# Sample queries spread per head inside the query product of a decoder trunk

## The chip, the cores and the metric

The kernel runs on one core of a Trainium2 chip. The core has five engines that run their own instruction lists and meet only at semaphores: PE (matrix products into PSUM banks), DVE and ACT (elementwise work), POOL and SP (here they mostly issue transfers). The metric is the device time of one launch in microseconds. Of the kernel before there are three runs: 1816.34, 1818.75 and 1823.96 us, median 1818.75 us.

## The reference, cut to what matters

Two token groups pass the same two layers: 256 prompt tokens and 8 sample tokens (one each of 8 sequences). Each layer has a token mixer, a cross attention over 256 memory tokens with 4 heads of 256 columns, and a channel mixer (dense, then eight experts). The prompt attends to keys computed in the kernel; each sample token attends to a cache of its own, read from memory:

```python
def cross_attention(h, k, v, w_q, w_o):
    b, s, _ = h.shape
    q = (h @ w_q).reshape(b, s, XATTN_HEADS, XATTN_HEAD_DIM)
    scores = jnp.einsum('bshd,bmhd->bhsm', q, k) * (XATTN_HEAD_DIM ** -0.5)
    p = jax.nn.softmax(scores, axis=-1).astype(v.dtype)
    o = jnp.einsum('bhsm,bmhd->bshd', p, v).reshape(b, s, D_MODEL)
    return o @ w_o

y_prompt = trunk(x_prompt, mem_k_prompt, mem_v_prompt, ...)   # 256 tokens, one memory
y_sample = trunk(x_sample, cache_mem_k, cache_mem_v, ...)     # 8 tokens, caches (2, 8, 256, 4, 256)
```

A layer's sample caches are 8 MB of keys and 8 MB of values. All data is fp32.

## The kernel before, in words

All 264 tokens (`T` = `TP` + `TS` = 256 + 8) are held transposed, features on the 128 partitions. Weights come in pieces of 1 MB through a ring of six slots (`raw`); ACT rounds a piece to fp32r (`whi`), DVE takes the remainder (`wlo`, in `split`), and PE multiplies hi by hi, hi by lo and lo by hi (`product`). `split(n + SPLIT)` for a piece three ahead stands in ACT's and DVE's lists behind the work on piece n. The order of each engine is the order of the code.

A layer's attention begins with the query product: four pieces, one head each (`q0` or `q1`, in `normed_product`). After the first piece stands a channel sum for the RMS norm (`channel_sum`, line 684). DVE scales each piece into `qT` (`q_out`, line 1657). Small results go through PSUM banks 4 to 7 in turn, by a running job number (`AUX`, `aux`, `job_out`): a job waits until the job four before it has been read.

Then, before the change, in this order:
- PE turns the sample queries into rows (`q_tok`), ACT copies them to `qs`; PE makes the prompt scores (`scores`, line 805), DVE takes their maxima (lines 1667, 1670), ACT the exponentials into `pr` (line 1223) and later the scaled `pr` (line 1231).
- For each sample s and each half of the columns PE spreads a query row over all partitions (`q_bc`, line 813: a column of the identity, held over 128 columns, times `qs`, 8 rows deep), and DVE multiplies it with the keys and sums (line 1685, four instructions a job, one for each head and half of the memory). There are 16 such jobs and 64 such instructions in a layer.
- PE turns the sample scores (`s_t`) and the prompt's probabilities (`p_t`), forms the prompt's output (`o_t`, line 838), and, with the values scaled by ACT (line 1248) and summed by DVE (line 1710), the samples' output (`s_o`, line 846). The product `o0` or `o1` follows.

POOL issues the cache loads (`load_caches`, line 505), 1 MB each, one sample's keys or values, in runs of 4 KB. Keys go through a ring of three slots (`kv`); values through it as well and through `va` (over `qT`) and `vb` (over `kT`), each of these two used twice in a layer.

Of the kernel before, what the change touches and what calls it, by code (L numbers as in the profile page):

```python
# [12 lines left out]
P = 128  # L13
# [3 lines left out]
TS = 8  # L17
# [106 lines left out]
for _c in range(CH):  # L124
    EP += [("g", _c, 0), ("g", _c, 1), ("u", _c, 0), ("u", _c, 1)]
    if _c:
# [16 lines left out]
_ATT = [("rms_xatt", 1), ("q_tok", 2), ("scores", 4), ("q_bc", 16), ("s_t", 1), ("p_t", 4), ("ps_t", 1), ("o_t", 4),  # L143
        ("s_o", 2), ("os_t", 1)]
for _name, _count in (
    [("vec", 1), ("mem_t", 4), ("x_t", 8), ("ws_t", 2), ("ws_0", 1), ("rms_mix0", 1), ("k_tok0", 4), ("ln_a0", 1), ("ln_b0", 1),
     ("v_smp", 2), ("v_tok", 4), ("mixed", 4)] + [(n + "0", c) for n, c in _ATT]
    + [("rms_ffn0", 1), ("rms_mix1", 1), ("state_t", 4), ("pconv", len(PE_CONV)), ("k_tok1", 4), ("ln_a1", 1), ("ln_b1", 1), ("c_tok", 4)]
    + [(n + "1", c) for n, c in _ATT] + [("ya", 3), ("route", 1), ("yb", 3), ("pos", 2)]
):  # L150
    AUX[_name] = _n
    _n += _count

# [31 lines left out]
def build_step(nc, ctx, a, out):  # L185
# [12 lines left out]
    def sem(name):  # L198
        return ctx.enter_context(nc.semaphore(name))
# [50 lines left out]
    vb = at("vb", [P, 2, D], F32, c_off + 8192)  # L250
    sc = at("sc", [P, 2, TS * HEADS], F32, e_off + 45312)
# [81 lines left out]
    v_scaled, v_summed, va_in, vb_in = sem("v_scaled"), sem("v_summed"), sem("va_in"), sem("vb_in")  # L333
# [57 lines left out]
    def key_slot(i, s):  # L391
        return ring_slot(12 * i + s)

    def value_slot(i, s):
        if s in (0, 5):
            return va[:, :, :], (va_in, 16 * (2 * i + s // 5 + 1))
        if s in (1, 6):
            return vb[:, :, :], (vb_in, 16 * (2 * i + s // 6 + 1))
        return ring_slot(12 * i + 8 + (2, 3, 4, 7).index(s))
# [5 lines left out]
    def job_out(name, j=0):  # L405

        n = AUX[name] + j
        return aux_free[n % 4], n // 4 + 1

    def job_bank(name, j=0):  # L410
        return bank[4 + (AUX[name] + j) % 4]
# [65 lines left out]
    def _(pool):  # L477
# [23 lines left out]
        def load_caches(i):  # L501

            def load(cache, s, place):
                dst, (loaded, _) = place
                pool.dma_start(dst, a[cache][i, s].rearrange("(m p) h d -> p m (h d)", p=P)).then_inc(loaded, 16)

            for s in range(TS):
                if s == 3:
                    pool.wait_ge(aux_ready, AUX[f"scores{i}"] + 4)
                    load("cache_mem_v", 0, value_slot(i, 0))  # L510
                    load("cache_mem_v", 1, value_slot(i, 1))
                if s >= 3:
                    pool.wait_ge(*job_out(f"q_bc{i}", 2 * (s - 3) + 1))
                elif i == 1 and s < 2:
                    pool.wait_ge(vused, s + 4)
                elif i == 1:
                    pool.wait_ge(aux_ready, AUX["s_o0"] + 2)
                load("cache_mem_k", s, key_slot(i, s))
            for s in range(2, TS):
                if s < 5:  # L520
                    pool.wait_ge(*job_out(f"q_bc{i}", 2 * (s + 3) + 1))
                else:
                    pool.wait_ge(vused, (TS - 1) * i + s - 4)
                load("cache_mem_v", s, value_slot(i, s))
# [109 lines left out]
    def _(pe):  # L634
        def aux(name, j=0):

            n = AUX[name] + j
            if n >= 4:
                pe.wait_ge(aux_free[n % 4], n // 4)
            return bank[4 + n % 4]  # L640
# [150 lines left out]
        def attention(i):  # L791
            normed_product(f"q{i}", 4, f"xatt{i}")
            pe.wait_ge(*stage_out(f"q{i}", 4))
            for j in range(2):
                y = aux(f"q_tok{i}", j)
                for kk in range(4):
                    mm = turn(y[0:TS, kk * P:(kk + 1) * P], qT[:, 4 * j + kk, TP:T], P)
                mm.then_inc(aux_ready, 1)
            for j in range(4):
                y = aux(f"scores{i}", j)  # L800
                tt, hh = j // 2, j % 2
# [6 lines left out]
            pe.wait_ge(*job_out(f"q_tok{i}", 0))  # L808
            pe.wait_ge(*job_out(f"q_tok{i}", 1))
            for s in range(TS):  # L810
                for c in range(2):
                    y = aux(f"q_bc{i}", 2 * s + c)
                    pe.matmul(y[:, :], ident[0:TS, s:s + 1].to_broadcast([TS, P]), qs[:, c * 512:(c + 1) * 512],  # L813
                              start=True, stop=True).then_inc(aux_ready, 1)
# [5 lines left out]
            for j in range(4):  # L820
                tt, mt = j // 2, j % 2
                y = aux(f"p_t{i}", j)
                pe.wait_ge(p_done, 4 * i + 2 * tt + 2)
# [259 lines left out]
    def _(act):  # L1083
# [24 lines left out]
        def job_copy(name, j, dst, rows_=P, cols=512):  # L1108
            act.wait_ge(aux_ready, AUX[name] + j + 1)
# [102 lines left out]
        def attention(i):  # L1212
            normed_pieces(f"q{i}", 4, f"xatt{i}")
            if i == 1:
                act.wait_ge(stored, 16 * 4)
            for j in range(2):
                job_copy(f"q_tok{i}", j, qs[:, j * 512:(j + 1) * 512], TS)
            for j in range(4):
                tt, hh = j // 2, j % 2
# [7 lines left out]
            for j in range(4):  # L1227
                act.wait_ge(rsum_done, 4 * i + j + 1)
                for h2 in range(2):
                    tt, h = j // 2, 2 * (j % 2) + h2  # L1230
# [224 lines left out]
    def _(dve):  # L1455
# [22 lines left out]
        def job_copy(name, j, dst, rows_=P, cols=512):  # L1478
            dve.wait_ge(aux_ready, AUX[name] + j + 1)
# [173 lines left out]
        def attention(i):  # L1653
# [6 lines left out]
            normed_pieces(f"q{i}", 4, f"xatt{i}", q_out)  # L1660
            if i == 1:
                dve.wait_ge(stored, 16 * 4)
            for j in range(4):
                tt, hh = j // 2, j % 2
                c = 4 * tt + 2 * hh
                dve.wait_ge(aux_ready, AUX[f"scores{i}"] + j + 1)
# [3 lines left out]
                dve.tensor_scalar(att[:, 8 + c:10 + c], att[:, c:c + 2], -SCALE, None, ALU.mult).then_inc(nmax_done, 1)  # L1670
            for j in range(4):
                tt, hh = j // 2, j % 2
# [3 lines left out]
            for s in range(TS):  # L1676
                keys, loaded = key_slot(i, s)
                dve.wait_ge(*loaded)
                for c in range(2):
                    j = 2 * s + c  # L1680
                    dve.wait_ge(aux_ready, AUX[f"q_bc{i}"] + j + 1)
                    for h in (2 * c, 2 * c + 1):
                        for mt in range(2):
                            k = keys[:, mt, h * HD:(h + 1) * HD]
                            ins = dve.tensor_tensor_reduce(k, k, job_bank(f"q_bc{i}", j)[:, (h % 2) * HD:(h % 2 + 1) * HD],
                                                           1.0, 0.0, ALU.mult, ALU.add,
                                                           sc[:, mt, s * HEADS + h:s * HEADS + h + 1])
                    ins.then_inc(job_out(f"q_bc{i}", j)[0], 1)
# [425 lines left out]
```

## Time and profile before

| | |
|---|---|
| median of three runs | 1818.75 us (1816.34 to 1823.96) |
| profiled execution | 1817.56 us, its span 1815.8 us |
| mean granted TensorE clock | 0.967 of full |
| busy share of the span | PE 95%, DVE 77%, ACT 59%, POOL 4% |
| chain that ended last | PE 90%, DVE 5%, ACT 2%, DMA 2% |
| attention of layer 0, from the channel sum's end to the first matmul of `o0` | 177.46 to 263.48 us |
| attention of layer 1, the same | 692.60 to 779.34 us |

The share of busy time counts PE as busy while a matmul waits in its pipeline, and the two attentions make up under a tenth of the span. So the stretches that the change touches are read by themselves: the chain of waits says in order of time which engine's work ended last, the timeline gives the length of single instructions and the distance between their starts, and the windows give the granted clock of a stretch.

### The profile page before, as it was taken

The page shows a single profiled execution, that of the slowest core. Times are in us where ns is not written, and L with a number is a line of the kernel's source. Part 1 is how long each engine was busy: PE and PEld are TensorE (multiplying, and loading weights), DVE is VectorE, ACT ScalarE, POOL GpSimd, SP SyncE. Part 2 cuts the span into 40 slices and gives each one's busy share as a digit, 9 for nine tenths or more (in the row PEclk, how much of TensorE's full clock was granted, in tenths as well). Part 3 has the DMA queues.
Part 4 walks back from the last instruction along what each step waited for, and adds up shares of the span by engine and source line. Part 5 has one row for each costly group of instructions (what it writes and reads, how often), then busy time and mean ns, then how long its engine had stood idle before and what let it go on. Part 6 is the DMA issues. An engine that isn't in the chain of part 4 may idle for free.

```text
span 1815.8 us, 23483 instructions
## 1 busy us (share of the span) xinstructions
PE 1733.5 (95%) x9598; PEld 1476.6 (81%) x9598; DVE 1400.5 (77%) x1635; ACT 1079.6 (59%) x1051; POOL 76.9 (4%) x86
## 2 busy tenths in 40 slices
PE   7998989999999989998999999999999999999996
PEld 6988659999999878486888888888888888888875
DVE  6566756665588966646888988988889889888896
ACT  4543344443454445335777777777777777777764
POOL 0000110000000000110000000000000000000000
PEclk9999789999999989688999999999999999999998
DMA  9644744555752345635999999999999999999993
GB/s 327 212 162 165 274 167 149 179 178 172 222 186 73 116 165 189 252 117 201 371 380 378 380 369 380 374 374 383 370 376 380 367 385 371 377 381 371 378 384 110
DMA packets 286375, 505.91 MB, mean 279 GB/s; under 512 B 8295, under 2 KB 100807, under 8 KB 285717
## 3 DMA queue, kind: packets, MB, share of 16 engines
q1 hardware_dynamic: 271904, 449.41, 70.1%
q0 software_dynamic: 13856, 54.75, 8.1%
q8 instruction: 78, 1.28, 0.3%
q14 instruction: 37, 0.30, 0.0%
q10 hardware_dynamic: 500, 0.18, 0.0%
HBM read 491.93 MB, written 13.33 MB: 278 GB/s over the span
## 4 chain that ended last, share of the span: by engine, by line
PE 90%; DVE 5%; ACT 2%; DMA 2%; issue 1%; ACTq 0%; DVEq 0%; POOLq 0%
PE bank L1028 17%; PE bank L1030 17%; PE bank L1029 16%; PE bank L668 9%; PE bank L669 9%; PE bank L670 9%; PE bank L692 3%; PE bank L735 2%; PE bank L684 2%; PE bank L813 1%; PE bank L838 1%; PE bank L661 1%; PE bank L663 1%; PE bank L662 1%; PE bank L805 1%
## 5 line engine op out<-in xcount | busy, mean ns | idle before, releaser
L1907 DVE TENSOR_TENSOR wlo<-raw,whi 128x2048 fp32r<-128x2048 f32 x333 | 761.9, 2289 | 110.1 <-ACT whi L1364 109.2
L1364 ACT ACTIVATE whi<-raw 128x2048 fp32r<-128x2048 f32 x333 | 638.6, 1918 | 211.0 <-PE bank L1030 211.0
L1028 PE MATMUL bank<-whi,xeh 128*128 128x512 f32 x896 | 360.9, 403 | 1.8 <-DVE wlo L1907 1.2
L1030 PE MATMUL bank<-whi,xel 128*128 128x512 f32 x896 | 352.5, 393 | 0.0
L1029 PE MATMUL bank<-wlo,xeh 128*128 128x512 f32 x896 | 349.0, 390 | 0.0
L668 PE MATMUL bank<-xh,whi 128*128 128x264 f32 (+1 forms) x1056 | 306.3, 290 | 19.0 <-DVE xl L1537 8.0
L1466 DVE TENSOR_TENSOR wlo<-raw,whi 128x2048 fp32r<-128x2048 f32 (+1 forms) x93 | 211.7, 2276 | 141.7 <-ACT whi L1096 141.3
L669 PE MATMUL bank<-xl,whi 128*128 128x264 f32 (+1 forms) x1056 | 302.4, 286 | 0.0
L670 PE MATMUL bank<-xh,wlo 128*128 128x264 f32 (+1 forms) x1056 | 302.1, 286 | 0.0
L1096 ACT ACTIVATE whi<-raw 128x2048 fp32r<-128x2048 f32 (+1 forms) x93 | 175.8, 1891 | 163.2 <-PE bank L670 161.7
L668 PEld LDWEIGHTS bank<-xh,whi 128*128 128x128 f32 x1056 | 202.2, 191 | 20.8 <-issue 16.3
L669 PEld LDWEIGHTS bank<-xl,whi 128*128 128x128 f32 x1056 | 202.4, 192 | 0.3
L670 PEld LDWEIGHTS bank<-xh,wlo 128*128 128x128 f32 x1056 | 201.5, 191 | 0.0
L1030 PEld LDWEIGHTS bank<-whi,xel 128*128 128x128 f32 x896 | 168.8, 188 | 39.2
L1028 PEld LDWEIGHTS bank<-whi,xeh 128*128 128x128 f32 x896 | 169.2, 189 | 34.8 <-DVE wlo L1907 2.5
L1029 PEld LDWEIGHTS bank<-wlo,xeh 128*128 128x128 f32 x896 | 169.2, 189 | 34.4
L1028 PE MATMUL bank<-whi,hTh 128*128 128x512 f32 x448 | 176.8, 395 | 1.9 <-DVE hTl L1949 1.9
L1030 PE MATMUL bank<-whi,hTl 128*128 128x512 f32 x448 | 175.6, 392 | 0.0
L1029 PE MATMUL bank<-wlo,hTh 128*128 128x512 f32 x448 | 174.0, 388 | 0.0
L1028 PEld LDWEIGHTS bank<-whi,hTh 128*128 128x128 f32 x448 | 84.2, 188 | 19.9 <-DVE wlo L1907 2.3
L1030 PEld LDWEIGHTS bank<-whi,hTl 128*128 128x128 f32 x448 | 84.1, 188 | 19.6
L1029 PEld LDWEIGHTS bank<-wlo,hTh 128*128 128x128 f32 x448 | 84.1, 188 | 18.6
(314 smaller groups left out, 1870.2 us busy)
## 6 DMA issues: line engine op xcount, KB each, us to landing
raw<-in_moe_w_gate SPq DMA_DIRECT2D x112, 1024.0 KB, 6.3
raw<-in_moe_w_up SPq DMA_DIRECT2D x112, 1024.0 KB, 6.9
raw<-in_moe_w_down SPq DMA_DIRECT2D x112, 1024.0 KB, 6.8
kv<-in_cache_mem_k POOLq DMA_DIRECT2D x16, 1024.0 KB, 5.5
raw<-in_b_w_pw SPq DMA_DIRECT2D x12, 1024.0 KB, 5.2
raw<-in_ffn_w_gate SPq DMA_DIRECT2D x11, 1024.0 KB, 5.3
raw<-in_ffn_w_up SPq DMA_DIRECT2D x11, 1024.0 KB, 5.3
raw<-in_w_xk SPq DMA_DIRECT2D x8, 1024.0 KB, 9.0
```

The source lines that it names most:

```text
L668: pe.matmul(y, w_hi[:, cols], x_hi, start=first, stop=False)
L669: pe.matmul(y, w_hi[:, cols], x_lo, start=False, stop=False)
L670: mm = pe.matmul(y, w_lo[:, cols], x_hi, start=False, stop=last)
L684: mm = pe.matmul(y[:, 0:T], ones[:, :], src[:, k, :], start=(k == order[0]), stop=(k == order[-1]))
L692: return pe.transpose(dst, src, ident[0:rows_, 0:rows_])
L1028: pe.matmul(y[:, :], x_hi, w_hi, start=starts, stop=False)
L1029: pe.matmul(y[:, :], x_hi, w_lo, start=False, stop=False)
L1030: mm = pe.matmul(y[:, :], x_lo, w_hi, start=False, stop=stops)
L1096: act.activation(whi[:, n % SPLIT, 0:w], raw[:, n % RAW, 0:w], ACT.Copy).then_inc(hi_done, 1)
L1364: act.activation(whi[:, n % SPLIT, :], raw[:, n % RAW, :], ACT.Copy).then_inc(hi_done, 1)
L1466: dve.tensor_tensor(wlo[:, n % SPLIT, 0:w], raw[:, n % RAW, 0:w], whi[:, n % SPLIT, 0:w].bitcast(F32), ALU.subtract).then_inc(lo_done, 1)
L1907: dve.tensor_tensor(wlo[:, n % SPLIT, :], raw[:, n % RAW, :], whi[:, n % SPLIT, :].bitcast(F32), ALU.subtract).then_inc(lo_done, 1)
```

## The change

The 16 spreading jobs are no longer one for each sample and half, but four for each head, two samples each, and they stand inside the query product: after pieces 1, 2 and 3 of it PE spreads the head of the piece before, and the last head between the two pairs of prompt scores. A job is now a 128x128 matrix of ones times four 128x128 diagonals (`dq`), which ACT writes from `qT` (64 instructions in a layer; the identity scaled by a column). `q_tok` and its copies to `qs` fall away. DVE's 64 score instructions are the same in number and size, and follow their head's spreading. The prompt scores go by pairs of heads, in order (head pair, token tile). Keys are loaded per head and four samples (1 MB, now in runs of 1 KB); values of samples 3 to 6 have the homes `va`, `vb`, `vc` (over `pr`) and `vm` to themselves, and 0, 1, 2 and 7 go through the ring.

```diff
-_ATT = [("rms_xatt", 1), ("q_tok", 2), ("scores", 4), ("q_bc", 16), ("s_t", 1), ("p_t", 4), ("ps_t", 1), ("o_t", 4),
-        ("s_o", 2), ("os_t", 1)]
+_ATT = [("rms_xatt", 1), ("q_bc", 12), ("scores_l", 2), ("q_bd", 4), ("scores_r", 2), ("s_t", 1), ("p_t", 4), ("ps_t", 1),
+        ("o_t", 4), ("s_o", 2), ("os_t", 1)]
...
+    vc = at("vc", [P, 2, D], F32, sq_off)
+    dq = at("dq", [P, 4, 4, P], F32, e_off + 8448)
...
+    def keys_free(i, r):
+        return job_out(f"q_bc{i}", 4 * (r // 2) + 2 * (r % 2) + 1)
...
     def value_slot(i, s):
...
+        if 3 <= s <= 6:
+            place, loaded = ((va, va_in), (vb, vb_in), (vc, vc_in), (vm, vd_in))[s - 3]
+            return place[:, :, :], (loaded, 16 * (i + 1))
+        return ring_slot(12 * i + 8 + (0, 1, 2, 7).index(s))
...
# POOL, load_caches
+            for r in range(8):
+                h, half = r // 2, r % 2
+                if r >= 3:
+                    pool.wait_ge(*keys_free(i, r - 3))
...
+            for s in range(TS):
+                if s < 3:
+                    pool.wait_ge(*keys_free(i, s + 5))
+                elif s < 5:
+                    pool.wait_ge(aux_ready, job_no(f"scores{i}", 3) + 1)
+                elif s == 5:
+                    pool.wait_ge(aux_ready, job_no(f"p_t{i}", 3) + 1)
+                elif s == 6:
+                    pool.wait_ge(vm_out, 16 * (i + 1))
+                    pool.wait_ge(aux_ready, job_no(f"o_t{i}", 3) + 1)
+                else:
+                    pool.wait_ge(vused, (TS - 1) * i + 1)
...
# PE, attention
+            def spread(h):
+                for jj in range(4):
+                    j = 4 * h + jj
+                    y = aux(f"q_bc{i}", j)
+                    pe.wait_ge(dq_done, 16 * i + j + 1)
+                    pe.matmul(y[:, :], ones[:, :], dq[:, jj, :, :].rearrange("p b n -> p (b n)"),
+                              start=True, stop=True).then_inc(aux_ready, 1)
...
+            for h in range(HEADS - 1):
+                product(f"q{i}", 1, x_hi, x_lo, start=h + 1)
+                spread(h)
...
+            scores(0)
+            scores(1)
+            spread(HEADS - 1)
+            pe.wait_ge(*stage_out(f"q{i}", 4))
+            scores(2)
+            scores(3)
...
# ACT, attention
+            def spread_rows(n):
+                h = n - FIRST[f"q{i}"]
+                act.wait_ge(*tile_out(n, 1))
+                for jj in range(4):
+                    j = 4 * h + jj
+                    if h > 0:
+                        act.wait_ge(aux_ready, job_no(f"q_bc{i}", j - 4) + 1)
+                    for b in range(4):
+                        s = 2 * jj + b // 2
+                        ins = act.activation(dq[:, jj, b, :], ident[:, :], ACT.Copy,
+                                             scale=qT[:, 2 * h + b % 2, TP + s:TP + s + 1])
+                    ins.then_inc(dq_done, 1)
...
+            for h in range(1, HEADS):
+                pieces(f"q{i}", 1, start=h)
+                spread_rows(FIRST[f"q{i}"] + h)
...
# DVE, attention
+            for h in range(HEADS):
+                n = FIRST[f"q{i}"] + h
+                q_out(n)
+                if h > 0:
+                    sample_scores(h - 1)
+                split(n + SPLIT)
+            largest(0)
+            largest(1)
+            sample_scores(HEADS - 1)
+            largest(2)
+            largest(3)
```

PE's list in layer 0, from the last prompt scores (`kT,qT`) on, before: the spreading jobs (`qs,ident`) stand one behind the other after all four scores.

```order
L805 MATMUL bank<-kT,qT 128x256 [waits aux2_free]
L805 MATMUL bank<-kT,qT 128x256 x3
L805 MATMUL bank<-kT,qT 128x256 [waits aux3_free]
L805 MATMUL bank<-kT,qT 128x256 x3
L813 MATMUL bank<-qs,ident 128x512 [waits aux0_free,aux3_free,aux2_free]
L813 MATMUL bank<-qs,ident 128x512 [waits aux1_free]
```

The same place after the change, from the third head's last two spreading jobs (`dq,ones`) on:

```order
L815 MATMUL bank<-dq,ones 128x512 [waits dq_done,aux0_free]
L815 MATMUL bank<-dq,ones 128x512 [waits dq_done,aux1_free]
L825 MATMUL bank<-kT,qT 128x256 [waits aux2_free,bank3_evac]
L825 MATMUL bank<-kT,qT 128x256 x3
L825 MATMUL bank<-kT,qT 128x256 [waits aux3_free]
L825 MATMUL bank<-kT,qT 128x256 x3
L815 MATMUL bank<-dq,ones 128x512 [waits dq_done,aux0_free]
L815 MATMUL bank<-dq,ones 128x512 [waits dq_done,aux1_free]
L815 MATMUL bank<-dq,ones 128x512 [waits dq_done,aux2_free]
L815 MATMUL bank<-dq,ones 128x512 [waits dq_done,aux3_free]
L825 MATMUL bank<-kT,qT 128x256 [waits aux0_free,bank3_evac]
```

The first three heads' jobs have moved ahead of the scores, and the last head's third and fourth job now wait for the banks (`aux2`, `aux3`) that hold the first two scores.

POOL's list in layer 0 from the fourth key load on, before (`kv`, `va`, `vb` are the places; `aux` banks come free when DVE has used a spread query, `vused` rises when PE has used a sample's values):

```order
L505 DMA kv<-in_cache_mem_k 128x2x1024 [waits aux1_free]
L505 DMA kv<-in_cache_mem_v 128x2x1024 [waits aux3_free]
L505 DMA kv<-in_cache_mem_v 128x2x1024 [waits aux1_free]
L505 DMA kv<-in_cache_mem_v 128x2x1024 [waits aux3_free]
L505 DMA va<-in_cache_mem_v 128x2x1024 [waits vused]
L505 DMA vb<-in_cache_mem_v 128x2x1024 [waits vused]
L505 DMA kv<-in_cache_mem_v 128x2x1024 [waits vused]
```

And after, from the last key load on:

```order
L525 DMA kv<-in_cache_mem_k 128x8x256 [waits aux3_free]
L541 DMA kv<-in_cache_mem_v 128x2x1024 [waits aux1_free] x2
L541 DMA kv<-in_cache_mem_v 128x2x1024 [waits aux3_free]
L541 DMA va<-in_cache_mem_v 128x2x1024 [waits aux_ready]
L541 DMA vb<-in_cache_mem_v 128x2x1024 [waits aux_ready]
L541 DMA vc<-in_cache_mem_v 128x2x1024 [waits aux_ready]
L541 DMA vm<-in_cache_mem_v 128x2x1024 [waits aux_ready,vm_out]
L541 DMA kv<-in_cache_mem_v 128x2x1024 [waits vused]
```

Three value loads waited for values used by PE; now one does, and it stands behind the load into `vm`, which waits for the last job of the prompt's output.

## Rows read from the trace of the kernel before

**Rows 1.** Chain of waits, layer 0: start us, length us, engine, tile, line, count

```profile
173.90 3.56 PE bank L684 x16
...
194.90 0.45 DVE qT L1657
...
196.42 6.92 PE bank L805 x32
...
204.34 1.03 ACT pr L1223 x4
...
207.03 20.79 PE bank L813 x24
...
229.35 4.04 PE bank L692 x18
...
234.06 9.04 PE bank L838 x32
...
249.25 6.54 DMA kv<-in_cache_mem_v
...
257.55 1.68 DVE kv L1710 x4
...
259.28 1.90 PE bank L846 x4
261.20 0.60 ACT qs L1110
...
263.48 0.35 PE bank L668
```

**Rows 2.** Chain of waits, layer 1

```profile
689.04 3.56 PE bank L684 x16
...
779.34 0.34 PE bank L668
```

**Rows 3.** Timeline of DVE, layer 0: start us, us, engine, line, operation, tiles, count

```profile
196.90 2.29 DVE L1466 TENSOR_TENSOR wlo<-raw,whi 128x2048 fp32r<-128x2048 f32 x1 [1.57 <-ACT whi L1096]
199.10 0.68 DVE L1667 TENSOR_REDUCE att<-bank 128x2 f32<-128x512 f32 x1
...
199.91 0.69 DVE L1667 TENSOR_REDUCE att<-bank 128x2 f32<-128x512 f32 x1
...
205.51 0.42 DVE L1685 CUSTOM_DVE_ANT_0 kv<-kv,bank 128x256 f32<-128x256 f32 x1
...
213.38 0.41 DVE L1685 CUSTOM_DVE_ANT_0 kv<-kv,bank 128x256 f32<-128x256 f32 x1
```

**Rows 4.** Timeline of ACT, layer 1: diagonals of the convolution, eight in a row

```profile
576.59 2.44 ACT L1294 ACTIVATE diag<-ident,vecs 128x128 f32<-128x128 f32 x8
```

**Rows 5.** Timeline of ACT, layer 0: scaled probabilities, and the values of three samples

```profile
205.26 3.29 ACT L1231 ACTIVATE pr<-pr,att 128x256 f32<-128x256 f32 x8
...
243.62 4.88 ACT L1248 ACTIVATE kv<-kv,sprob 128x256 f32<-128x256 f32 x12
```

**Rows 6.** Windows: stretch, us, busy (count) of PE, PEld, DVE, ACT, POOL, PEclk, DMA, GB/s

```profile
178.00:195.00 17.00, 16.86 (x140) 16.64 (x138) 11.36 (x12) 3.88 (x3) 0.00 (x0) 1.00 0.44 139
208.00:236.00 28.00, 26.11 (x49) 12.64 (x48) 21.44 (x121) 5.29 (x13) 5.62 (x8) 0.50 0.92 341
546.00:636.00 90.00, 85.06 (x556) 78.55 (x555) 78.62 (x174) 43.48 (x104) 0.76 (x1) 1.00 0.28 94
642.00:644.00 2.00, 0.00 (x0) 0.00 (x0) 1.97 (x6) 0.00 (x0) 0.00 (x0) 1.00 0.93 263
644.00:646.00 2.00, 1.46 (x4) 1.18 (x5) 2.00 (x6) 0.00 (x0) 0.00 (x0) 0.51 1.04 415
```

**Rows 7.** DMA issues: tiles, queue, count, KB each, median us to landing

```profile
raw<-in_w_xq SPq DMA_DIRECT2D x8, 1024.0 KB, 5.0
...
out_conv_s<-in_state_conv POOLq DMA_DIRECT2D x1, 928.0 KB, 13.3
```

**Rows 8.** All instructions on the tile kv (cache loads): time to landing

```profile
DMA to landing us min/median/max: 5.2/5.4/10.0
```

More of the change, by code:

```diff
@@ L152, with job_no @@
     _n += _count
+def job_no(name, j=0):
+    kind = name[:-1]
+    if kind == "q_bc" and j >= 12:
+        return AUX["q_bd" + name[-1]] + j - 12
+    if kind == "scores":
+        return AUX[("scores_l", "scores_r")[j // 2] + name[-1]] + j % 2
+    return AUX[name] + j
 XW = {n: 8 * i for i, n in enumerate(["mix0", "mixed", "xatt0", "att0", "ffn0", "mix1", "mem1", "conv", "xatt1", "att1"])}
@@ L791, in attention, with scores @@
         def attention(i):
[L792 to L799, printed above, removed]
+            def spread(h):
[5 more added lines that the diff above has]
+                              start=True, stop=True).then_inc(aux_ready, 1)
+            def scores(j):
                 y = aux(f"scores{i}", j)
-                tt, hh = j // 2, j % 2
+                hh, tt = j // 2, j % 2
                 for h2 in range(2):
@@ L807, in attention @@
                 mm.then_inc(aux_ready, 1)
[L808 to L814, printed above, removed]
+            product(f"q{i}", 1, x_hi, x_lo, (x_done, XW[f"xatt{i}"]))
+            channel_sum(f"rms_xatt{i}", sq, {0: [(sq_done, SQ[f"xatt{i}"])]})
+            for h in range(HEADS - 1):
+                product(f"q{i}", 1, x_hi, x_lo, start=h + 1)
+                spread(h)
+            pe.wait_ge(*tile_out(FIRST[f"q{i}"] + 1, 1))
+            scores(0)
[4 more added lines that the diff above has]
+            scores(3)
             pe.wait_ge(*job_out(f"q_bc{i}", 15))
@@ L1658, in q_out, with sample_scores, largest @@
                         .then_inc(tile_out(n, o)[0], 1)
[L1660 to L1664, printed above, removed]
+            def sample_scores(h):
+                for half in range(2):
+                    keys, loaded = key_slot(i, 2 * h + half)
+                    keys = keys.rearrange("p m d -> p (m d)").rearrange("p (s m d) -> p s m d", s=4, m=2)
+                    dve.wait_ge(*loaded)
+                    for jj in range(2):
+                        j = 4 * h + 2 * half + jj
+                        dve.wait_ge(aux_ready, job_no(f"q_bc{i}", j) + 1)
+                        for s2 in range(2):
+                            s = 4 * half + 2 * jj + s2
+                            for mt in range(2):
+                                k = keys[:, 2 * jj + s2, mt, :]
+                                ins = dve.tensor_tensor_reduce(k, k, job_bank(f"q_bc{i}", j)[:, s2 * HD:(s2 + 1) * HD],
+                                                               1.0, 0.0, ALU.mult, ALU.add,
+                                                               sc[:, mt, s * HEADS + h:s * HEADS + h + 1])
+                        ins.then_inc(job_out(f"q_bc{i}", j)[0], 1)
+            def largest(j):
+                hh, tt = j // 2, j % 2
                 c = 4 * tt + 2 * hh
-                dve.wait_ge(aux_ready, AUX[f"scores{i}"] + j + 1)
+                dve.wait_ge(aux_ready, job_no(f"scores{i}", j) + 1)
                 own(dve.tensor_reduce(att[:, c:c + 2], job_bank(f"scores{i}", j)[:, :].rearrange("p (h m) -> p h m", h=2),
```

77 lines of the change are left out of this document (23 added, 54 removed).

## Prediction

> **What bounds the kernel now.** I read the busy shares first, then the chain of waits through both attentions, then the timelines of DVE and ACT there, the windows for the granted clock, and last the transfers. Over the span PE ends last, so a change counts where PE stands waiting, or where it works for something that DVE does later. The reader is to see that in the 86.0 us of layer 0's attention (from the channel sum's end, 173.90 + 3.56 = 177.46, to the first matmul of `o0`, 263.48) [rows 1]. Up to 194.90 the query product fills PE; then come scores and softmax, and from about 205.5 to 229.35 the sample scores, with the spreading matmuls (L813) and DVE's L1685 in step. From 229.35 the probabilities are turned, from 234.06 to 243.1 the prompt's output is formed, and the last 20 us are the samples' values, with a load of 6.54 us on the chain. Layer 1 is the same in 779.34 − 692.60 = 86.7 us [rows 2].
>
> In the query product DVE is busy 11.4 of 17.0 us and ACT 3.9 of 17.0, with the granted clock at 1.00 [rows 6]. A head's sample scores are 16 of the 64 L1685 instructions. The first and the 24th of a row without gaps start at 205.51 and 213.38 [rows 3], so one takes 0.342 us and a head 5.5 us, 5.8 with the waits between its jobs.
>
> **The change, in layer 0's times.** Durations are those of the profiled execution.
>
> *Query product.* A piece is 48 matmuls (8 row blocks, 2 halves, 3 products). 140 take 16.86 us at full clock [rows 6], so a piece takes 5.8 us. A spreading job is two PE instructions of 512 columns; 16 of 264 columns take 3.56 us, also with the ones as stationary side [rows 1], so 512 take 0.432 us and a head's four jobs 3.45 us. The other end is the pace of the old jobs at half clock, 20.79 / 24 = 0.87 us an instruction [rows 1], 6.9 us a head. I take 3.45, because the product ran at clock 1.00. Three pieces and two heads' spreading come before the last piece's end: 177.46 + 17.4 + 6.9 = 201.8.
>
> *The diagonals.* ACT's eight diagonals of the convolution took 2.44 us [rows 4], so 16 take 4.9. With a weight piece, of which ACT's 3.88 us held two [rows 6], that is under 7 us a head, against 9.25 us of PE for a piece and its spreading: hidden. Only head 0 is close, whose diagonals wait for the norm as well and are wanted one piece later. If this cover is gone, it costs 4.9 us a layer at most.
>
> *DVE sets the end.* Between two pieces DVE has two `q_out` (0.9) [rows 1], 5.8 us of scores and a split of 2.3 [rows 3]: 9.0 against PE's 9.25, so heads 0 and 1 are hidden. Behind the last piece it works without a gap: `q_out` to 202.4; head 2's scores to 208.2; the split, to 210.5; two maxima, 0.81 us apart [rows 3], to 212.1; head 3's scores to 217.9; two maxima to 219.5. Here the change adds a wait: head 3's third and fourth job need the banks of the first two prompt scores, which ACT reads only after DVE's maxima. ACT ends the first pair of exponentials at 211.3 + 1.03 = 212.4 [rows 1], the job is spread by 213.3, and DVE comes to it at 212.1 + 2.8 = 214.9. That wait is covered by 1.6 us. Queued behind it on PE are the last scores, which DVE asks for at 217.9 and which are 3.5 us of work from 215: covered, closely.
>
> *Softmax and the turns.* Exponentials of the last job and a reciprocal take 1.2 us, to 220.7, and the eight scalings 3.29 [rows 5], to 224.0; before, these lay beside the sample scores, and now they stand on the path. The turns start with the third of the four pairs (223.2) and take 16/18 of 4.04, 3.6 us, to 226.8; the last copy takes 0.60, to 227.4.
>
> *Prompt output.* 9.04 us before [rows 1], begun at the clock of 0.50 granted up to 236 [rows 6]; 32 instructions of the same 256 columns took 6.92 in the scores [rows 1]. Those are the two ends. I take 9.04: between the last scores, near 218.5, and the turns at 223.2 PE has only the sample scores to turn. An idle PE was set back before: it did nothing from 642 to 644, and the next two us were granted 0.51 [rows 6]. The Trainium skill, "TensorE: Matmul & The Clock Gate", section "HAM oscillation — how this bites in real kernels", says that short bursts of matmuls between waits start at half rate again each time. By that rule the sum is the one given here; without it, it is the first rival's. The rows agree with it. So the output ends at 236.4.
>
> *Values.* ACT copies the last output (0.6, to 237.0) and scales samples 2 to 7 at 4.88 / 3 = 1.63 us each [rows 5], to 246.8; DVE 1.7, PE 1.9, and 2.3 from there to the first matmul of `o0` (261.20 to 263.48) [rows 1]: 252.7. The load that was on the chain goes if the last two loads arrive in time: into `vm` from 236.4, then sample 7 from 237.1. At the median landing of 5.4 us [rows 8] they are there at 241.8 and 242.5, and ACT wants them at 243.5 and 245.1.
>
> *Keys.* The fourth block's slot comes free when two jobs of head 0 are read (183.3 + 0.9 + 2.8 = 187.0), and the block is wanted in the midst of head 1 (192.5 + 0.6 + 2.8 = 195.9): 8.9 us, and as much for the sixth and eighth. Runs of 1 KB on POOL's queue are not in the trace. The lower end is 5.0 us, the query weights, in runs of 1 KB but from SP's queue; the upper is 13.3, the longest 1 MB transfer on POOL's queue, memory to memory [rows 7]. I take 5.4, as the caches have now, which is nearest in queue and place: hidden. The Trainium skill, "SBUF — State Buffer", section "🔬 SBUF: two separate sides", holds that a POOL-issued transfer can stall on its descriptors while DVE keeps the port the two share. If that cost a split's length here, a key load would take 7.7 us and stay hidden; a late last value load would cost 0.6 us. No row here isolates it, and it only adds to the chance of the second rival.
>
> *Sum.* Layer 0 ends at 252.7 instead of 263.48: 10.8 us. The same 75.2 us in layer 1 against 86.7 saves 11.5. The profiled execution of 1817.56 would be 1795.3; it lies 1.2 us under the median, so 1818.75 − 22.3 = 1796.5 us. Later stages only shift: the weight ring holds the same six pieces when `o0` and `o1` begin.
>
> **Rivals.**
> - *The prompt's output runs at full clock.* For it: up to 218 PE also has spreading and scores of 128 rows, which the old kernel had not. Against: the row at 644. It saves 9.04 − 6.92 = 2.1 us a layer more: 1792.3.
> - *The last value loads come late.* They are issued after the last prompt output, later in the chain than before. At the longest landing seen, 10.0 us [rows 8], sample 6 is there at 246.4 instead of the 243.5 wanted, and sample 7 at 247.1, hidden behind it: 2.9 us a layer, 1802.3. If key loads also took 13.3, three blocks in a layer would be 4.4 us late each, 26 us in all, and nothing would be left: about 1823. For the first: up to three loads are in flight together. Against: SP has filled its six slots by then and waits.
> - *Slower: the spreading costs PE its clock.* From 208 to 236, mostly old spreading, PE counts as busy 26.1 of 28.0 us, and yet the granted clock is 0.50 [rows 6]. If the ones times diagonals did the same, from the first spreading on, two pieces (11.6 us) and one head's spreading (3.45) would be added before the last piece's end, and after it PE's 13.8 us of spreading and scores would be 27.6, against DVE's 17.1: 10.5 more. 25.6 − 11.2 is 14.4 us a layer lost: 1847. It decides from about 11 us a layer, that is 22 us of PE work at half clock. Against: the old jobs were 8 rows deep, the new are 128; the convolution's matmuls with diagonals ran at 1.00 for 90 us [rows 6], and the channel sum's ones kept the product at 1.00.
>
> **How the numbers follow.** Forecast 1796.5, chance 0.55, its own range 1793 to 1801. Full clock (1792.3) 0.20. Late values (near 1802) 0.13, with late keys too, no gain, 0.06. Clock lost, slower, 0.06. For the range I leave out the slower case and the late keys. On the low side full clock less 2.4 us, the distance of the lowest of the three runs from their median, gives 1790, and I take 1789; on the high side late values and the highest run's 5.2 us give 1808. A measurement of this kernel tells some 0.5%, 9.1 us, from no change, so faster means under 1809.7: 0.55 + 0.20 + 0.13 = 0.88. The late keys divide between no change (0.05) and slower (0.01), and the lost clock makes it 0.07 for slower.
>
> **What would show it.** Right: L1685's groups between the pieces, matmuls of the pieces at 0.12 us with 1.00 granted, some 18 us of DVE without a gap behind the last piece, the output starting near 227.5, ACT scaling six samples without waiting for a transfer, and attentions of about 75 us. Wrong: a wait of DVE on `kv` loads, a clock of 0.50 inside the product, ACT waiting for `vm` or `kv`, or PE waiting for `dq`.

## The result, and the profile after

| kernel | median us (runs) | ratio to the kernel before, 95% interval |
|---|---|---|
| before | 1820.73 (4) | 1 |
| changed | 1796.56 (1795.65 to 1800.82; 4) | 0.9869 [0.9852, 0.9886] |

With a fourth run (1822.71 us) the median of the kernel before is 1820.73 us; the prediction started from 1818.75, the median of three. Predicted were 1796.5 us and a range of 1789 to 1808. The profiled execution of the changed kernel took 1795.65 us, 21.9 less than the profiled one of before. In it the attentions of the two layers, from the channel sum's end to the first matmul of `o0` and `o1`, are 75.6 and 75.9 us long (75.2 was forecast) instead of 86.0 and 86.7 [rows 1, 2]: 21.2 of the 21.9 us are there.

The chain of waits through layer 0 after the change (start, length, engine, tile, line, count), with what stood in [rows 1] shifted by the new lines: L701 is the channel sum, L685 to L687 the product, L815 the spreading, L1712 the sample scores, L709 the turns, L864 the prompt's output, L872 the values.

```profile
173.04 3.56 PE bank L701 x16
...
182.40 3.43 PE bank L815 x8
...
200.86 0.87 PE bank L815 x2
201.87 0.42 DVE kv L1712
...
207.42 2.20 DVE wlo L1505
...
217.73 1.93 ACT pr L1262 x8
219.66 2.38 ACT pr L1270 x6
...
222.18 3.66 PE bank L709 x16
...
226.51 8.96 PE bank L864 x32
...
236.10 1.60 ACT kv L1287 x4
...
239.45 10.48 PE bank L872 x24
...
252.23 0.34 PE bank L685
```

The 24 spreading instructions that took 20.79 us in a row [rows 1] are gone from the stretch behind the scores; 16 of them stand between the pieces, at 0.43 us each, and no transfer is on the chain. The ends of layer 1's attention, in the same view:

```profile
677.93 3.56 PE bank L701 x16
...
757.41 0.34 PE bank L685
```

The windows of layer 0 after (stretch, length, busy time and count of PE, PEld, DVE, ACT, POOL, then granted clock, DMA share, GB/s):

```profile
176.60:201.00 24.40, 24.40 (x161) 20.38 (x161) 22.28 (x76) 18.40 (x52) 3.53 (x4) 1.00 0.72 235
201.00:218.00 17.00, 14.17 (x50) 8.75 (x48) 16.36 (x73) 10.02 (x27) 3.27 (x5) 1.00 1.01 344
218.00:222.00 4.00, 0.00 (x0) 0.00 (x0) 1.21 (x8) 4.00 (x15) 1.12 (x2) 0.74 1.03 398
222.00:228.00 6.00, 5.48 (x22) 4.78 (x23) 0.78 (x4) 5.12 (x13) 0.71 (x1) 0.50 0.93 332
228.00:235.50 7.50, 7.50 (x31) 6.14 (x30) 5.24 (x11) 3.63 (x8) 0.00 (x0) 0.86 0.34 134
235.50:252.30 16.80, 14.68 (x41) 3.29 (x40) 11.73 (x33) 11.12 (x27) 1.41 (x2) 1.00 0.33 125
```

PE works without a pause at 1.00 through the product, where DVE is now busy 22.3 of 24.4 us (11.4 of 17.0 before [rows 6]). It stands still for 4 us at 218, and behind that the clock is 0.50. DVE's timeline from the last piece on (accumulator reads left out; the brackets give the idle time before an instruction and what ended it):

```profile
201.87 0.42 DVE L1712 CUSTOM_DVE_ANT_0 kv<-kv,bank 128x256 f32<-128x256 f32 x1 [0.54 <-PE bank L815]
...
207.34 2.29 DVE L1505 TENSOR_TENSOR wlo<-raw,whi 128x2048 fp32r<-128x2048 f32 x1
...
217.44 0.68 DVE L1722 TENSOR_REDUCE att<-bank 128x2 f32<-128x512 f32 x1
...
223.30 0.15 DVE L1752 RECIPROCAL att<-att 32x1 f32<-32x1 f32 x1 [2.96 <-ACT psm L1275]
```

Up to 218.4 there is no gap, and none of its waits names a load of `kv`; then it waits for ACT's exponentials and scalings. ACT's timeline, with diagonals (`dq`), weight pieces (`whi`) and the last two samples' values:

```profile
179.79 4.79 ACT L1249 ACTIVATE dq<-ident,qT 128x128 f32<-128x128 f32 x16 [2.68 <-DVE qT L1696]
184.49 1.90 ACT L1122 ACTIVATE whi<-raw 128x2048 fp32r<-128x2048 f32 x1
...
242.37 1.70 ACT L1287 ACTIVATE vm<-vm,sprob 128x256 f32<-128x256 f32 x4
244.31 1.70 ACT L1287 ACTIVATE kv<-kv,sprob 128x256 f32<-128x256 f32 x4 [0.24 <-DMA kv<-in_cache_mem_v]
```

### The profile page after: what moved, and what is told of

Read it like the earlier page. It is cut to its first block, busy times and chain, and to the rows that moved or that the text cites. A ratio compares the mean times of both kernels' runs of the same rounds, so it can differ in the third digit from the quotient of the medians.

```text
span 1793.9 us, 23613 instructions
## 1 busy us (share of the span) xinstructions
PE 1707.6 (95%) x9582; PEld 1468.1 (82%) x9582; DVE 1399.1 (78%) x1635; ACT 1114.1 (62%) x1175; POOL 82.0 (5%) x86
## 4 chain that ended last, share of the span: by engine, by line
PE 90%; DVE 5%; ACT 3%; issue 1%; DMA 1%; ACTq 0%; DVEq 0%; POOLq 0%
PE bank L1054 17%; PE bank L1056 17%; PE bank L1055 16%; PE bank L685 9%; PE bank L686 9%; PE bank L687 9%; PE bank L709 3%; PE bank L752 2%; PE bank L701 2%; PE bank L872 1%; DVE kv L1712 1%; PE bank L864 1%; PE bank L815 1%; PE bank L678 1%; PE bank L680 1%
## 5 line engine op out<-in xcount | busy, mean ns | idle before, releaser
L685 PE MATMUL bank<-xh,whi 128*128 128x264 f32 (+1 forms) x1056 | 308.1, 292 | 19.0 <-DVE xl L1576 8.0
L687 PE MATMUL bank<-xh,wlo 128*128 128x264 f32 (+1 forms) x1056 | 302.1, 286 | 0.0
L685 PEld LDWEIGHTS bank<-xh,whi 128*128 128x128 f32 x1056 | 202.1, 191 | 21.8 <-issue 17.3
L687 PEld LDWEIGHTS bank<-xh,wlo 128*128 128x128 f32 x1056 | 201.5, 191 | 0.0
```

What stands on the lines that cost most here:

```text
L685: pe.matmul(y, w_hi[:, cols], x_hi, start=first, stop=False)
L687: mm = pe.matmul(y, w_lo[:, cols], x_hi, start=False, stop=last)
```

## The experiments

Each ratio is to runs of the kernel before on the same chip (their medians lie between 1818.62 and 1820.73 us). "Attention" is the length defined above, in the profiled execution, layer 0 and layer 1.

| kernel | median us | ratio, 95% interval | attention, us |
|---|---|---|---|
| old homes | 1806.55 | 0.9929 [0.9916, 0.9943] | 80.2, 79.5 |
| homes only | 1810.88 | 0.9954 [0.9940, 0.9967] | 82.4, 82.4 |
| diagonals twice | 1830.47 | 1.0061 [1.0047, 1.0075] | 93.0, 92.7 |
| eight rows | 1814.53 (one run) | | 85.7, 83.4 |
| deep, in the old place | 1817.14 | 0.9994 [0.9982, 1.0006] | 85.8, 86.4 |
| late split | 1790.77 | 0.9842 [0.9828, 0.9855] | 76.4, 71.3 |
| busy PE | 1793.47 | 0.9856 [0.9840, 0.9871] | 73.7, 73.0 |
| scores first | 1790.21 | 0.9845 [0.9832, 0.9859] | 72.2, 72.2 |
| scores first, busy PE | 1788.03 | 0.9823 [0.9808, 0.9837] | 71.6, 71.5 |
| the same with an early slot | 1787.19 | 0.9832 [0.9815, 0.9849] | 71.7, 71.5 |
| changed, again | 1799.20 | 0.9876 [0.9856, 0.9896] | 75.7, 75.8 |
| scores first, busy PE, again | 1787.92 | 0.9816 [0.9798, 0.9834] | 72.3, 71.3 |

### The two halves of the change apart

**Old homes:** the changed kernel, with the value caches where they were (the loads' order and waits go back with them).

```diff
-        if 3 <= s <= 6:
-            place, loaded = ((va, va_in), (vb, vb_in), (vc, vc_in), (vm, vd_in))[s - 3]
-            return place[:, :, :], (loaded, 16 * (i + 1))
-        return ring_slot(12 * i + 8 + (0, 1, 2, 7).index(s))
+        if s in (0, 5):
+            return va[:, :, :], (va_in, 16 * (2 * i + s // 5 + 1))
+        if s in (1, 6):
+            return vb[:, :, :], (vb_in, 16 * (2 * i + s // 6 + 1))
+        return ring_slot(12 * i + 8 + (2, 3, 4, 7).index(s))
```

> The changed kernel with the value caches in their old places and old load order (va and vb twice, the rest in the ring); keys per head and the spreading in the product stay. My theory is that the homes are worth what the tail behind the prompt's output lost: 20.4 us before, 16.7 after, so 3.6 us a layer comes back and the time is about 1804; the trace should show ACT waiting some 6 us for a value load again. Rival: the homes are worth nothing by themselves, since a load in the ring would come in time now too: 1796.5. Second rival: the homes made most of the gain, since the late load also holds the keys of the next layer: 1812 or more.

The load is back on the chain of layer 0, behind the first sample that frees a place:

```profile
239.86 1.90 PE bank L868 x4
...
242.04 7.37 DMA kv<-in_cache_mem_v
...
257.09 0.34 PE bank L681
```

1806.55 is 2.5 us over the theory's 1804. The sizes per layer are 4.5 and 3.6 us instead of 3.6 and 3.6; ACT waited 1.78, 1.08 and 1.88 us for three loads in layer 0, not 6 us for one. A part lies behind layer 0's attention, where its length does not show it: the product of `o0` started at a clock of 0.71 (1.00 in the changed kernel), and from its first matmul to the next channel sum it took 32.6 us instead of 31.0. The window of its start:

```profile
257.10:263.00 5.90, 5.90 (x36) 5.90 (x37) 0.80 (x6) 0.00 (x0) 3.42 (x4) 0.71 0.39 156
```

**Homes only:** the kernel before, with the same homes for samples 3 to 6 (the same edit as the lines with a minus above, and the loads' waits).

> The kernel before with nothing but the new value homes (samples 3 to 6 in va, vb, vc and vm). My theory: the load on the chain goes and about 3.6 us a layer are saved, 1820.7 - 7.3 = 1813.5, and this gain and that of the spreading alone add up to the whole of about 24 us. Rival: the values wait for another load, at the old place in the program, and nothing is gained: 1820.

The values run without a gap in both layers, here in layer 1:

```profile
760.81 10.48 PE bank L847 x24
```

Of the 172.8 us of both attentions before, the homes alone save 8.0 and the rest alone 13.1. That is about 21, and together they saved 21.2. So the two halves hardly touch one another, and the spreading in the product is worth the larger one.

### What the spreading needs

**Diagonals twice.** ACT writes each diagonal two times; what PE reads is unchanged.

```diff
+                        own(act.activation(dq[:, jj, b, :], ident[:, :], ACT.Copy,
+                                           scale=qT[:, 2 * h + b % 2, TP + s:TP + s + 1]))
+                    own.settle()
+                    for b in range(4):
+                        s = 2 * jj + b // 2
                         ins = act.activation(dq[:, jj, b, :], ident[:, :], ACT.Copy,
```

> The changed kernel with every diagonal written twice by ACT, one set behind the other: 32 instead of 16 a head, some 4.9 us more of ACT each. With the weight piece (1.9) ACT then has 11.5 us a head, against 9.25 us of PE, so the cover I counted on is gone. My theory: it costs about 2.3 us for each of three heads, and with head 0's, wanted at once, up to 4.9 more, so 5 to 12 us a layer, 1807 to 1820, with PE waiting for dq. Rival: the spreading has more slack than that, because DVE's sample scores are what each head waits for, and it costs little: under 1801.

33.9 us over the changed kernel's first median, 17 a layer, and so past my 12. The chain of layer 0 shows why:

```profile
180.29 1.29 ACT dq L1249 x4
...
224.23 1.28 ACT dq L1254 x4
...
225.52 1.28 ACT L1267
...
226.82 1.03 ACT pr L1267 x4
...
227.89 3.41 PE bank L815 x4
```

From 180.29 to 226.82 nearly all of it is ACT: four heads' diagonals of 9.9 us, three weight pieces of 1.8 and a table load. I had priced three heads' excess. Behind the fourth head's diagonals, though, ACT's queue holds the exponentials that free the banks for that head's own third and fourth job (227.89), and these begin 49.7 us behind the channel sum's end, 15.9 later than in the changed kernel (210.46, 33.9 us behind it). The cover itself is thin for head 0: in the changed kernel its last diagonal ends at 179.79 + 4.79 = 184.58, and PE comes to it three jobs into its spreading, 182.40 + 6 x 0.43 = 184.98.

**Eight rows.** The spreading multiplies 8 of the 128 rows; the other 120 rows of each diagonal are left out of the sum.

```diff
-                    pe.matmul(y[:, :], ones[:, :], dq[:, jj, :, :].rearrange("p b n -> p (b n)"),
+                    pe.matmul(y[:, :], ones[0:TS, :], dq[0:TS, jj, :, :].rearrange("p b n -> p (b n)"),
```

> The changed kernel with the spreading's stationary and moving side cut to 8 of 128 rows (120 of the 128 rows of each diagonal are left out of the sum), same columns, same number of instructions. If the depth of 8 rows is what held the clock at 0.50 in the old spreading, matmuls behind each spreading fall to half clock, the product grows by up to 11.6 us and the time goes to between 1805 and 1847. Rival: the old stretch was slow for its pauses and small tiles, not for its rows, and between full pieces 8 rows keep 1.00: 1796.5.

The theory of the depth holds. A piece, a spreading, the next piece, and the third spreading with the first scores:

```profile
188.00:195.00 7.00, 7.00 (x49) 6.85 (x48) 5.18 (x18) 4.55 (x16) 1.76 (x2) 0.82 0.76 259
195.00:200.00 5.00, 5.00 (x10) 1.77 (x10) 4.19 (x22) 4.86 (x12) 0.64 (x1) 0.74 0.81 271
200.00:207.80 7.80, 7.80 (x49) 7.65 (x49) 4.43 (x14) 1.73 (x6) 1.12 (x2) 0.73 0.85 286
207.80:218.40 10.60, 10.60 (x26) 6.50 (x25) 8.96 (x36) 8.63 (x21) 1.59 (x2) 0.68 0.69 240
```

PE is busy in every microsecond, and yet the clock is 0.68 to 0.82; pieces that took 5.8 us take 7.3 to 8.4. The values between 0.50 and 1.00 are means: behind the first spreading the piece's matmuls stand 0.22 us apart up to 190.7, and 0.12 from there on. It is one run, but it lies 18.0 us over the changed kernel's median, whose four runs spread over 5.2. This was my slower rival, at a smaller price, since the clock was down only part of the time: its mechanism is real, and 128 rows are what kept the change out of it. The attentions together save 3.7 us against the kernel before, less than the homes alone (8.0).

**Deep, in the old place.** The kernel before, its old spreading with 128 rows, 120 of them zeros.

```diff
-                    pe.matmul(y[:, :], ident[0:TS, s:s + 1].to_broadcast([TS, P]), qs[:, c * 512:(c + 1) * 512],
+                    pe.matmul(y[:, :], ident[:, s:s + 1].to_broadcast([P, P]), qs_all[:, c * 512:(c + 1) * 512],
```

> The kernel before with one thing changed: its spreading matmuls, in their old place behind the scores, multiply 128 rows instead of 8 (the other 120 are zeros, written by ACT while the query product runs). If eight rows are what held the granted clock at 0.50 there, it is 1.00 from the sample scores on: the spreading leaves the chain to DVE (64 scores of 0.342 us, 21.9 us, about 2 us less), and the prompt's output takes 6.9 us instead of 9.0: 4 us a layer or a little more, about 1811. That would also say how much of the change's gain could be had without moving the work: under half. Rival: the clock fell for the pauses between the spreading matmuls, which stay, and it remains at 0.50: 1820.

The clock rose as the theory says, though not throughout, and the time did not follow. The windows of the spreading and of the turns in layer 0, and of the spreading in layer 1:

```profile
204.50:214.00 9.50, 8.23 (x17) 2.30 (x15) 8.56 (x52) 4.21 (x12) 2.28 (x4) 1.00 0.92 340
217.00:222.60 5.60, 5.41 (x8) 1.80 (x8) 4.70 (x29) 0.00 (x0) 1.40 (x2) 0.70 0.78 293
230.50:235.00 4.50, 4.35 (x20) 3.83 (x20) 1.16 (x6) 2.69 (x6) 0.70 (x1) 0.53 1.00 397
719.50:744.00 24.50, 16.16 (x31) 4.43 (x29) 22.46 (x132) 4.21 (x12) 5.85 (x9) 0.99 0.94 348
```

The same stretch stood at 0.50 before [rows 6]; the 0.70 follows a wait of PE of 1.87 us. But DVE has 21.9 us of sample scores there in any case, and gets ahead of the key loads (idle time in brackets):

```profile
215.68 0.42 DVE L1689 CUSTOM_DVE_ANT_0 kv<-kv,bank 128x256 f32<-128x256 f32 x1 [1.54 <-DMA kv<-in_cache_mem_k]
...
222.14 0.42 DVE L1689 CUSTOM_DVE_ANT_0 kv<-kv,bank 128x256 f32<-128x256 f32 x1 [0.90 <-DMA kv<-in_cache_mem_k]
```

And while it finished alone, PE stood from 226 to 230.5 and the clock was low again for the turns. The prompt's output behind them took 7.19 us in layer 0 but 9.46 in layer 1 (9.04 and 9.30 before), and a value load is still on the chain of both layers. So the depth is needed, and is worth nothing where it was: place and depth gain only together.

### What sets the end now

**Late split.** One of DVE's weight splits goes from ahead of the last head's scores to where DVE waits 2.96 us for ACT (up to 223.30 in its timeline above).

```diff
-                split(n + SPLIT)
+                if h < HEADS - 1:
+                    split(n + SPLIT)
...
+            split(FIRST[f"q{i}"] + HEADS - 1 + SPLIT)
```

> The changed kernel with one of DVE's weight splits (2.2 us, the one between the third and the fourth head's sample scores) moved behind the samples' maxima, where DVE stands idle while ACT scales the probabilities. If DVE's unbroken work behind the last piece sets the end, 2.2 us a layer go: about 1792. Rival: PE's spreading and scores set the end, 1796.5 and a DVE that waits for PE. Second rival: the weight piece comes too late for the output product, above 1796.5.

The median, 1790.77, is 5.8 us below the changed kernel's first (0.9842 against 0.9869, and 0.9876 when measured again). Layer 1 of the profiled run saved 4.6: the split's 2.2, and 1.9 because the prompt's output ran in 7.19 us there. That run was the longest of the five (1796.22). In its layer 0 the turns began only 0.4 us earlier than in the changed kernel: DVE came to the last block of keys at 211.9 instead of 213.9 and waited 1.69 us for its load. A value load follows behind the output, and both are on the chain:

```profile
205.09 8.47 DMA kv<-in_cache_mem_k
...
237.53 7.90 DMA kv<-in_cache_mem_v
```

So what the split gave in that layer went to loads. And in both layers the product behind the attention started at a lower clock, 0.71 and 0.73 in its first 5.8 us (1.00 in the changed kernel), which the attention's length does not show.

**Busy PE.** Eight matmuls of the channel sum's kind, result unused, behind the turn of the sample scores, where PE stood still.

```diff
+            for k in range(KT):
+                pe.matmul(bank[0][:, 0:T], ones[:, :], hT[:, k, :], start=True, stop=True)
             for j in range(4):
                 tt, mt = j // 2, j % 2
                 y = aux(f"p_t{i}", j)
```

> The changed kernel with eight more channel-sum matmuls (264 columns, fp32, 3.6 us, result unused) where PE stands idle while ACT scales the probabilities. If the idle PE is what takes the clock, the turns and the prompt's output run at 1.00: 6.9 us instead of 9.0, and 2.1 us a layer less, about 1792. Rival: the turns alone hold the clock down (their moving side is 128 columns, with waits between) and it stays at 0.50 to 0.86: 1796.5. Second rival: the matmuls stretch past the wait and delay the turns: above 1797.

In the windows that had 0.74, 0.50 and 0.86 the clock is now

```profile
218.00:222.00 4.00, 4.00 (x21) 3.39 (x20) 2.13 (x10) 2.61 (x10) 1.81 (x3) 1.00 1.01 401
222.00:228.00 6.00, 4.34 (x29) 3.47 (x28) 0.90 (x5) 6.00 (x16) 0.71 (x1) 1.00 1.03 376
228.00:235.00 7.00, 7.00 (x32) 5.32 (x31) 5.29 (x12) 4.60 (x11) 0.25 (x1) 1.00 0.37 146
```

and the output takes 7.19 and 7.17 us instead of 8.96 and 9.10. The attentions become 2.0 and 2.9 us shorter, the median falls by 3.1 (the two intervals overlap). The output began 48.6 us behind the channel sum's end in layer 1 (49.9 in the changed kernel), but 49.7 in layer 0. There the clock was 0.73 behind an earlier pause of PE, the 2.07 us in which the last spreading waits for banks; the scores came late, and DVE waited 0.30 and 0.83 us for them. The changed kernel has the same pause, and kept 1.00 behind it in both layers.

**Scores first.** The late split, and all four prompt scores ahead of the last head's spreading, so that the softmax lies beside the last sample scores. PE's part (DVE's maxima and reciprocals move with it):

```diff
-            spread(HEADS - 1)
             pe.wait_ge(*stage_out(f"q{i}", 4))
             scores(2)
             scores(3)
+            spread(HEADS - 1)
```

> The late split, and besides all four prompt scores ahead of the last head's spreading, with their maxima and reciprocals ahead of and within that head's sample scores. By my theory the exponentials and the eight scalings (222.18 less 218.3, about 3.9 us) then lie beside sample scores; the turns begin right behind DVE's last sample score, near 216.5 instead of 222.18: 5.7 us a layer, about 1785. Rival: the last head's spreading now waits for banks that the exponentials free, DVE stands idle for it, and what is left is the split alone, 1792 or more.

3.5 and 3.7 us a layer against the changed kernel, 7.1 in all, where I expected 11.4. By the medians it can't be told from the late split alone (1790.21 and 1790.77, the intervals overlap), so its own worth is not shown; the rival, that nothing but the split's gain is left, is not ruled out. The softmax is off the chain, the turns begin at 218.54 instead of 222.18 (4.1 us earlier, counted from the channel sum's end), but not at 216.5: DVE waits for the last two scores, 0.49 and 0.83 us, and its reciprocals stand within its row.

```profile
209.99 0.69 DVE L1724 TENSOR_REDUCE att<-bank 128x2 f32<-128x512 f32 x1 [0.49 <-PE bank L825]
...
211.72 0.69 DVE L1724 TENSOR_REDUCE att<-bank 128x2 f32<-128x512 f32 x1 [0.83 <-PE bank L825]
```

**Scores first, busy PE:** seven unused matmuls in the 3.4 us that PE waits for DVE's last score.

> All prompt scores ahead of the last head's spreading and the late split, as in the kernel that ran at 1790.2, and seven unused channel-sum matmuls (264 columns, fp32, 3.1 us) in the 3.4 us in which PE waits there for DVE's last sample scores. If idle PE takes the clock, the turns and the output of the prompt run faster: 9.25 to 6.9 and 4.04 to some 2.5, 3 to 4 us a layer, about 1783. Rival: the clock stays, 1790.

1788.03, and 1787.92 when measured again beside the changed kernel (1799.20): 11 us less, intervals apart. From the late split and the scores first alone it is not told apart beyond doubt: their intervals touch its first one. It did not reach 1783. The late split now stands on the chain of both layers, and PE waits 1.50 us for what follows it, behind the turns. The output behind that pause took 7.10 us at 1.00 in layer 1, but 8.79 in layer 0 (8.79 and 7.11 when measured again); its first stretch in layer 0:

```profile
225.20:229.00 3.80, 3.80 (x12) 3.10 (x12) 1.90 (x7) 3.41 (x9) 0.00 (x0) 0.60 1.03 401
```

And the attention ends no sooner than 71.5 us, because the last value load is on the chain; split and load of layer 0:

```profile
222.15 2.20 DVE wlo L1507
...
236.13 7.48 DMA kv<-in_cache_mem_v
```

**With an early slot:** the first sample's matmuls go ahead of the last output job, so that this load's place comes free sooner.

```diff
             for j in range(4):
+                if j == 3:
+                    summed(0, 1)
                 y = aux(f"o_t{i}", j)
```

> The kernel with the prompt scores first and the unused matmuls (1788.0), and besides the first sample's four matmuls ahead of the last of the prompt's four output jobs, so that the ring slot which the last ring load waits for comes free before the prompt's output is done instead of behind it (sample 6 takes that slot, sample 7 the place of the prompt's values; one sample is scaled a job earlier on ACT and DVE). In that kernel's trace the last value load stands on the chain of both layers, and ACT waits 0.9 us for it in layer 0. My theory: the values' matmuls then run without a gap, 1 us saved in layer 0 and 2 in layer 1, about 1785. Rival: the load into the place of the prompt's values, which can't start earlier, is late in its stead: 1788. Second rival: the two output banks are not free in time and the output is held up: above 1788.

It came out as the first rival has it: the load into the prompt's values' place, which can't begin before the output is done, is late in its stead.

```profile
234.39 7.36 DMA vm<-in_cache_mem_v
```

Nothing is gained that can be measured (0.9832 against 0.9823 and 0.9816).

**Changed, and scores first with busy PE, again**, side by side:

> The changed kernel once more, so that the kernels derived from it can be compared on one chip in one stretch of time: 1796.6, as first measured, or a ratio of 0.987 to the kernel before. If chips or hours differ by more than 0.2%, the differences of 2 to 8 us between the variants mean nothing.

> The kernel with the prompt scores first, the late split and the seven unused matmuls, beside the changed kernel: 1788, some 8 us below it, if the first measurement holds; the rival is that the variants only differed by chip, and both come out alike.

Both held: the changed kernel came out at 0.9876 (0.9869 at first), the other at 0.9816 (0.9823). The two measurements of a kernel differ by under 0.1%, so the variants' differences of 5 us and more are theirs; smaller ones stay unclear.

## Why the prediction was right, point by point

The mechanism came out as forecast; that the number did to 0.1 us is luck. The four runs spread over 5.2 us, the same kernel gave 1799.20 when measured again, and from the median of four runs before the saving is 24.2 us, where 22.3 were forecast (21.9 between the profiled executions).

- *Query product.* Pieces of 5.8 us and heads' spreading of 3.43 (3.45 forecast) at 1.00. From the channel sum's end to the last piece's end 24.26 us (24.3). That the clock would hold rested on depth and on the channel sum's ones; the run with eight rows shows that depth decided.
- *Diagonals hidden.* Right, with 0.4 us to spare for head 0. The price without cover, 4.9 us a layer at most, counts one head's diagonals. The doubled ones took the cover from all four heads and cost 17 (5 to 12 were expected), because ACT's exponentials are queued behind them, and PE's last spreading waits for the banks that these free; what head 0's cover alone is worth was not measured.
- *DVE sets the end.* 16.5 us without a gap (201.87 to 218.4) against 17.1; in layer 1 of the late split, 2.2 us less of DVE in this row and 1.9 of clock make up 4.1 of the 4.6 saved. The added wait on banks was covered, as forecast.
- *Softmax and turns.* On the path, 217.73 to 222.18. Counted from the channel sum's end, the turns began 45.6 us later (45.7 forecast), the output 49.9 (49.9).
- *Prompt output.* 8.96 and 9.10 for 9.04, and 8.97 and 9.11 when measured again. The first rival, full clock, did not occur in the changed kernel's two profiles, but was near: PE kept busy gives 7.19. In layer 1 of the late split the pause ahead of the turns was 4.34 us, the turns ran at 0.57, and the output, at 1.00 from its start, in 7.19: how far the low clock reaches into it varies. The rule of the Trainium skill that the prediction named ("TensorE: Matmul & The Clock Gate", "HAM oscillation — how this bites in real kernels"), that matmuls after a wait start at half rate, agrees with these rows for the turns: 0.50 and 0.57 behind 4 us of idle PE, 1.00 without them. The run with eight rows is another case: PE never waited there.
- *Values.* Here a term was right in sum and not in kind. I let ACT's 1.63 us a sample set the pace; in the chain it is PE, 24 matmul instructions in 10.48 us without a gap, 1.75 a sample. From the output's end to the first matmul of `o0` it is 16.8 us instead of 16.3, and that is where layer 0's attention is longer than forecast (75.6 for 75.2).
- *Value loads.* In time, but ACT waited 0.24 us for the last. The rival of late loads was closer than its 0.13: four of the faster variants have such loads on the chain, 7.2 to 9.0 us long. Loads into `kv` land at a median of 6.7 us after the change against 5.4 [rows 8], so the figure I used was too kind. DVE never waited for keys in the changed kernel; 2.2 us earlier, in layer 0 of the late split, it did.

The remaining 0.7 us (21.9 less 21.2) lie ahead of layer 0's attention, which begins 0.9 us sooner (176.60 for 177.46); the stretches between the attentions and behind them are equal within 0.2 us. Why it begins sooner stays open.

## What to carry to other kernels

Work that two engines share is hidden only under a stage that leaves both engines room, and here also the transfers: deeper matmuls in the old place raised the clock and gained nothing, the move with eight rows lost most of the gain, and the two together saved 13 us. When a wait goes from a tail, ask at once which transfer is next late by how much; here ACT already waited 0.24 us for the last load, hidden behind PE's own values, and four of the variants that saved time ahead of it gave a part back to a load. The price of a lost cover includes what is queued behind the covered work on its engine.

## What the runs showed of the hardware

- Where the spreading used 8 of the 128 rows, PE counted as busy and the granted clock was low all the same: PE was busy 26.1 of 28.0 us at 0.50 in the kernel before [rows 6], and without a pause at 0.68 to 0.82 with eight rows in the product. With 128 rows and pauses of 0.24 us between pairs it was 1.00 while PE was busy 8.2 of 9.5 us.
- The turns run at 0.50 or 0.57 where PE stood still for 4 us ahead of them, and at 1.00 where unused matmuls fill that pause, at no cost that shows. Behind shorter pauses it varied: 2.07 us was followed by 1.00 in five cases read here and by 0.73 in one, 1.87 us by 0.70, and 1.50 us by 0.60 in layer 0 and 1.00 in layer 1 of the same kernel, in both its profiles.
- A key load in runs of 1 KB took POOL 0.88 us to issue, a value load 0.70, also where a DVE split ran beside it. From 186 to 215 us key loads landed in 7.0 us (5.2 before), but two of the weight loads there took 7.5 instead of 5.3 as well, so whether the shorter runs or the fuller queues slowed the keys stays open.
